# Two chained blocks on one core: 80 units of the modulation taken from the matrix engine and computed beside the feed-forwards

## The chip, the core and the metric

The kernel runs on one core of a Trainium2 chip. Five things work side by side in it: TensorE (PE, with its weight loads as PEld), VectorE (DVE), ScalarE (ACT), GpSimd (POOL, unused here), and the DMA queues, of which SyncE's (SP) brings nearly all weights. The metric is the device time of one execution in microseconds (us); lower is better.

## What is computed

256 tokens of width 1024 pass through two blocks, one after the other, in fp32.

```python
def first_block(x, ...):                 # two layers
    for layer in range(2):
        p = rms_norm(h, g1) @ w_in       # split into branch A, B, C and gates
        y_a = rwkv7_branch(p_a, ...)     # a recurrence, computed in chunks
        y_b = hgrn2_branch(p_b, ...)
        y_c = dsa_branch(p_c, ...)
        branch = einsum('bsnc,ncd->bsnd', [y_a, y_b, y_c], w_branch)
        h = h + (sum over n of sigmoid(p_gate) * branch) @ w_o
        u = rms_norm(h, g2)
        h = h + conv_glu(u, w_up, conv_w, conv_b, w_down)    # width 2816

def second_block(x, c, ...):             # two layers
    cond = silu(c)                       # one vector of 1024
    for layer in range(2):
        mod = cond @ ada_w[layer] + ada_b[layer]             # 1024 x 6144
        sh1, sc1, g1, sh2, sc2, g2 = split(mod, 6)
        h = rms_norm(x, ...) * (1 + sc1) + sh1
        x = x + g1 * hybrid_mixer(h, ...)  # GLA (log_a = f(ga @ w_alpha)) and retention
        h = rms_norm(x, ...) * (1 + sc2) + sh2
        x = x + g2 * (swiglu(h) if layer == 0 else moe_swiglu(h))  # 8 experts, top 2
    return rms_norm(x, final_g)
```

The product `cond @ ada_w` needs nothing of the first block: it can be made anywhere before the second block starts.

## The kernel before

**Products.** An fp32 product is made of three matmuls on rounded halves: w_high × u_high, w_high × u_low and w_low × u_high. The weights come in units of 128 x 1024 (512 KB). A unit of 8 K-tiles and 128 outputs takes 24 matmuls of 128x256. SyncE brings each unit into one of `RING` = 6 slots; ScalarE rounds it to `w_high` (`high_to`, L1744), VectorE subtracts (`low_to`, L2275, `w_low`), and TensorE multiplies (`project`, `mm3`, all recorded at L801). The halves live in 6 slots of their own (`SPLIT`), so a unit can be cut up to 6 ahead of its product. SyncE issues the loads in the order of the list `ORDER.loads`, and waits before each until the slot's former unit has been read: for a split unit by VectorE's cut, for a raw one ("r") by TensorE's product. Every engine runs its own program in the order in which it is written, and the waits are on semaphores that the others count up.

**The modulation.** `ada_w` of both layers is 96 units. TensorE multiplies them raw, in plain fp32, 48 in branch A of each layer of the first block (`mod_point`, L897). There A runs through some fifty short products of 64x64 tiles, each of which depends on the copies of the one before; at each `point()` four units stand between, with two matmuls of 512 columns for each (rows "bank<-ring,cond"). The results stand in PSUM bank 7. After 16 units (a round of `Rounds`) ScalarE copies the bank, TensorE transposes it at the next point ("const,rope"), and ScalarE takes 16 columns of `mod` out of it. At the end of branch B VectorE copies `mod` to `raw_mod`.

**Merge.** `branch(n, ...)` multiplies the outputs of A, B and C with 4 units each, 0 in banks 0 to 3, 1 and 2 both in banks 4 to 7; branch n's results are multiplied with gate n by VectorE ("taken", "merged") before their bank is free. Branch 2 waits for `gated` (VectorE), its high half (ScalarE, `high_y2`) and its low half (`cut2`). The units of w_o follow, in banks 0 to 7 in order, four of them interleaved by `begin`, and the sums of squares for the next norm.

**Feed-forward.** There are 22 groups of two up units (gate, value) and one down unit. Units are numbered in TensorE's order: `feed(j, n, groups)`; TensorE runs up of group j and then down of group j − 2. ScalarE and VectorE start group j with cutting up to `fed_ahead(j)` = 3j + 4 (5 for j = 0). In a conv group ScalarE then takes gate and value with the first tap (L2065, L2066), VectorE adds the two other taps (4 instructions, L2316), ScalarE makes the sigmoid (L2068), VectorE the two products (L2307), ScalarE `hid_high` (L2074) and VectorE `hid_low`. The third dense feed-forward (second block, layer 0) has no taps. At the end ScalarE cuts three units of the next stage (`ahead`), loads an activation table (L1777) and squares the new residual (L1780) for the norm, which TensorE sums.

**GLA.** `ga`, 16 columns of the projection, is made of 16 thin fp32 matmuls from constant weights ("const 128*16"). VectorE copies it, and TensorE makes `alpha` of it.

## Time and profile before

| | |
|---|---|
| median of 3 runs | 2419.52 us (2409.2 to 2420.85) |
| the profiled execution, its own time | 2427.1 us |
| its span in the profile | 2425.6 us |
| mean granted TensorE clock | 0.962 of full speed |
| busy: TensorE / VectorE / ScalarE | 2269.0 / 1601.5 / 1174.7 us |
| instructions: PE matmul / DVE / ACT | 19011 / 2442 / 1703 |

The profile comes from one execution, so its times are compared with each other and with its own total. A row of the timeline gives start, duration, engine, line and operation, and in brackets how long the engine had been idle before and what released it. "issue" is idle time for which nothing that the profile shows was waited for.

### The profile page before, as it was taken

How to read it: one execution, taken by the hardware profiler on the slowest of the kernel's cores; microseconds unless marked ns; L12 is line 12 of the kernel's file. 1: busy time of each engine (PE TensorE's matmuls, PEld its weight loads, DVE VectorE, ACT ScalarE, POOL GpSimd, SP SyncE). 2: the span in 40 equal slices, each digit the busy share in tenths (PEclk: the TensorE clock that was granted, in tenths of full speed). 3: DMA queues.
4: the chain of work that ended last, by engine and by line, in shares of the span. 5: the costliest groups of instructions: out<-in, count | busy, mean ns of one | idle time of the engine just before them, and what ended most of it. 6: DMA issues, size and time to landing. Idle time of an engine off the chain costs nothing.

```text
span 2425.6 us, 44884 instructions
## 1 busy us (share of the span) xinstructions
PE 2269.0 (94%) x19011; PEld 2047.3 (84%) x19011; DVE 1601.5 (66%) x2442; ACT 1174.7 (48%) x1703; POOL 0.2 (0%) x4
## 2 busy tenths in 40 slices
PE   7889998999998898989999989999989999999998
PEld 7569888999976798988998989998987888877776
DVE  6537976677673589576876666555666454577886
ACT  5234644555452455355554445444345344456665
POOL 0000000000000000000000000000000000000000
PEclk9999998999899999899998989999998999999999
DMA  5664433365447543253653325553313555579885
GB/s 209 229 252 165 139 122 121 114 200 198 137 163 256 206 138 123 88 172 123 205 188 130 131 82 179 184 187 130 126 36 133 180 200 176 175 278 321 328 319 198
DMA packets 118635, 427.06 MB, mean 176 GB/s; under 512 B 13345, under 2 KB 16161, under 8 KB 118305
## 3 DMA queue, kind: packets, MB, share of 16 engines
q1 hardware_dynamic: 116016, 421.81, 50.3%
q8 instruction: 150, 2.46, 0.4%
q10 hardware_dynamic: 2416, 2.37, 0.3%
q14 instruction: 53, 0.43, 0.1%
HBM read 423.08 MB, written 1.05 MB: 175 GB/s over the span
## 4 chain that ended last, share of the span: by engine, by line
PE 80%; DVE 11%; ACT 4%; issue 2%; DMA 2%; SPq 0%; ACTq 0%; DVEq 0%
PE bank L801 79%; DVE arena L2307 3%; DVE w_low L2275 3%; DMA ring<-in_weights 2%; DVE arena L2316 1%; ACT w_high L1744 1%; DVE y_mix L2307 1%; ACT arena L2024 1%; PE bank L1629 1%; DVE arena L2326 0%; DVE arena L2311 0%; PE bank L949 0%; DVE x_res L2316 0%; ACT arena L1750 0%; DVE u_low L2307 0%
## 5 line engine op out<-in xcount | busy, mean ns | idle before, releaser
L2275 DVE TENSOR_TENSOR w_low<-ring,w_high 128x1024 fp32r<-128x1024 f32 x700 | 822.9, 1219 | 144.9 <-ACT w_high L1744 143.9
L801 PE MATMUL bank<-u_high,w_high 128*128 128x256 f32 x2576 | 742.4, 288 | 36.8 <-DVE u_low L2307 19.7
L1744 ACT ACTIVATE w_high<-ring 128x1024 fp32r<-128x1024 f32 x700 | 700.9, 1051 | 134.4 <-PE bank L801 124.3
L801 PE MATMUL bank<-u_low,w_high 128*128 128x256 f32 x2576 | 734.1, 285 | 0.0
L801 PE MATMUL bank<-u_high,w_low 128*128 128x256 f32 x2576 | 733.5, 285 | 0.0
L801 PEld LDWEIGHTS bank<-u_high,w_high 128*128 128x128 f32 x2576 | 498.8, 194 | 50.8 <-issue 35.0
L801 PEld LDWEIGHTS bank<-u_low,w_high 128*128 128x128 f32 x2576 | 498.6, 194 | 0.1
L801 PEld LDWEIGHTS bank<-u_high,w_low 128*128 128x128 f32 x2576 | 497.8, 193 | 0.0
L801 PE MATMUL bank<-arena 64*64 64x64 f32 (+5 forms) x4456 | 232.8, 248 | 43.2 <-issue 21.5
L801 PEld LDWEIGHTS bank<-arena 64*64 64x64 f32 (+2 forms) x4456 | 204.0, 152 | 79.7 <-issue 57.1
L801 PE MATMUL bank<-w_high,u_high 128*128 128x256 f32 (+1 forms) x480 | 165.2, 344 | 0.0
L801 PE MATMUL bank<-w_low,u_high 128*128 128x256 f32 (+1 forms) x480 | 162.3, 338 | 0.0
L2307 DVE TENSOR_TENSOR arena<-arena 128x256 f32<-128x256 f32 (+3 forms) x218 | 141.8, 666 | 31.0 <-ACT arena L2068 21.3
L801 PE MATMUL bank<-w_high,u_low 128*128 128x256 f32 (+1 forms) x480 | 162.2, 338 | 0.0
L801 PE MATMUL bank<-hid_high,w_high 128*128 128x256 f32 x528 | 148.1, 280 | 1.0 <-DVE w_low L2275 1.0
L801 PE MATMUL bank<-hid_low,w_high 128*128 128x256 f32 x528 | 147.9, 280 | 0.0
L801 PE MATMUL bank<-hid_high,w_low 128*128 128x256 f32 x528 | 147.9, 280 | 0.0
L2307 DVE TENSOR_TENSOR turned_low<-bank,turned_high 128x256 fp32r<-128x256 f32 (+1 forms) x66 | 24.8, 399 | 158.3 <-ACT turned_high L2180 158.3
L2180 ACT ACTIVATE turned_high<-bank 128x256 fp32r<-128x256 f32 (+1 forms) x66 | 22.2, 365 | 218.3 <-PE bank L1629 218.3
L2316 DVE SCALAR_TENSOR_TENSOR arena<-bank,params,arena 128x255 f32<-128x255 f32 (+1 forms) x204 | 85.4, 475 | 39.7 <-ACT arena L2066 23.3
L1750 ACT ACTIVATE arena<-bank 128x512 f32<-128x512 f32 (+1 forms) x72 | 42.0, 583 | 138.2 <-PE bank L801 138.1
L801 PE MATMUL bank<-w_high,turned_high 128*128 128x512 f32 x242 | 99.7, 412 | 8.3 <-DVE w_low L2275 7.0
(307 smaller groups left out, 3062.7 us busy)
## 6 DMA issues: line engine op xcount, KB each, us to landing
ring<-in_weights SPq DMA_DIRECT2D x534, 512.0 KB, 4.5
ring<-in_moe SPq DMA_DIRECT2D x264, 512.0 KB, 5.2
const<-in_const SPq DMA_DIRECT2D x1, 2619.0 KB, 16.7
out<-x_res ACTq DMA_DIRECT2D x2, 512.0 KB, 3.0
x_res<-in_x SPq DMA_DIRECT2D x1, 512.0 KB, 5.1
x_res<-in_x ACTq DMA_DIRECT2D x1, 512.0 KB, 5.6
const<-in_par ACTq DMA_DIRECT2D x1, 462.0 KB, 3.4
params<-in_par ACTq DMA_DIRECT2D x1, 247.0 KB, 10.3
```

What stands on the lines that cost most here:

```text
L801: return pe.matmul(out, lhsT, rhs, start=start, stop=stop, skip_group_check=loose)
L1629: ins = pe.transpose(bank(q, tile)[:, f * P:(f + 1) * P], hid_e[q % 2][tile][:, f * P:(f + 1) * P], c_("ident"))
L1744: act.activation(WH[:, ORDER.slot[cut], :], weights("s", cut), Copy).then_inc(s_hi, 1)
L1750: act.activation(job.dst, held(job), Copy).then_inc(s_out["act"], 1)
L2024: act.activation(L_c[a][:, h, :], L_c[a][:, h, :], Exp, bias=neg_max[a][:, h:h + 1], accum_out=exp_sum[a][:, h:h + 1]).then_inc(*c.mark(f" ...
L2180: act.activation(HTH[q % 2][tile][:, 0:n], psum[4 + 2 * (q % 2) + tile][:, 0:n], Copy)\
L2275: dve.tensor_tensor(WL[:, b, :], weights("s", cut), WH[:, b, :].bitcast(f32), SUB).then_inc(s_lo, 1)
L2307: dve.tensor_tensor(out, a, b, op).then_inc(*t.mark(name))
L2316: dve.scalar_tensor_tensor(out, a, s, b, op0, op1).then_inc(*t.mark(name))
```

## The change

1. Of the 96 units of the modulation only round 0 of layer 0 (16 units) stays on TensorE in branch A; layer 1's A has none. The other 80 are laid out by result: a row of 128 x 1024 holds 128 columns' weights, one column to a partition. `ROWS` gives 20, 20 and 40 of them to the three dense feed-forwards. From group 3 on VectorE multiplies such a row with `cond_row` (the vector cond in all partitions) and ScalarE sums it up with a copy and `accum_out` into a column of `raw_mod`. Each of the three loads c, broadcast, as one unit more (kind "m"), and makes `cond_row` of it in groups 1 and 2. The slot of a row is free when VectorE's product is made.
2. In a conv group both engines have a new order. ScalarE: gate and value with taps, two highs, sigmoid, one high, `hid_high`, the sum of the group before. VectorE: taps, one low, the two products, one low, `hid_low`, one low, the modulation's product. In the third feed-forward the old order stays, and the rows' products stand ahead of `hid_low`.
3. Merge: branch 2 goes to banks 0 to 3, the units of branch 2 are cut further before its input is ready, gate 2 stands ahead of `high_y2`, and w_o goes to the banks `MIXED_BANK` = (7, 4, 5, 6, 0, 1, 2, 3), after `taken13`.
4. GLA: `ga` becomes a unit like the others (24 matmuls, a load and both cuts), the first in the mixer; `alpha` follows directly on VectorE's copy, and the other projection jobs come after it.

```diff
+    ROUNDS1 = range(0, 1), range(1, 1)
+    ROWS = range(16, 36), range(36, 56), range(56, 2 * MOD_UNITS)
+    GA2, QK2, RQK2, RV2, GV2, GR2, RG2, OUT2, FEED2 = 0, 1, 5, 13, 17, 21, 25, 29, 37
...
+    def _feed(self, g, first):
+        for j in range(FF_GROUPS):
+            before, last = self.fed_ahead(j - 1, FF_GROUPS) if j else -1, self.fed_ahead(j, FF_GROUPS)
+            self._load("s", first + before + 1, last - before)
+            of = self.modulated(g, j)
+            self._load("m", self.row1(g) + of[0] if len(of) else 0, len(of))
+
+    def modulated(self, g, j):
+        n = len(self.ROWS[g])
+        if j < 3:
+            return range(j == 1)
+        return range(1 + n * (j - 3) // (FF_GROUPS - 3), 1 + n * (j - 2) // (FF_GROUPS - 3))
...
                     if m == 0:
                         pe.wait_ge(*G.dve(f"cut{n}"))
+                        if n == 2:
+                            pe.wait_ge(*B.dve("gated"))
                     pe.wait_ge(s_lo, s + 1)
                     for dt in range(KT):
-                        if m == 0 and n == 2 and dt % 2 == 0:
-                            pe.wait_ge(*G.dve(f"taken1{dt // 2}"))
-                        ins = mm3(half((0, 4, 4)[n] + dt // 2, dt), halves(s, slice(dt * P, (dt + 1) * P)),
+                        ins = mm3(half((0, 4, 0)[n] + dt // 2, dt), halves(s, slice(dt * P, (dt + 1) * P)),
...
+            pe.wait_ge(*G.dve("taken13"))
+            begin(G.dve, [(s + dt, psum[MIXED_BANK[dt]][:, 0:T], True) for dt in range(4)])
+            projected_out(s, R, MIXED_BANK)
...
             high_to(s0 + ORDER.BRANCH + 7)
+            gate(2)
+            high_to(s0 + ORDER.BRANCH + 9)
             act.wait_ge(*B.dve("gated"))
             act.activation(YH[2], OUTS[2], Copy).then_inc(*g.mark("high_y2"))
-            gate(2)
...
+            def row(j):
+                K, at = of_rows[g], ORDER.row1(g)
+                if j == 1:
+                    act.wait_ge(*arrived("m", at))
+                    act.activation(cond_row, weights("m", at), Sigmoid).then_inc(*K.act.mark("cond"))
+                for i in ORDER.modulated(g, j) if j > 2 else ():
+                    act.wait_ge(*K.dve(f"product{i}"))
+                    col = ORDER.ROWS[g][i - 1]
+                    act.activation(products[i % 3], products[i % 3], Copy, accum_out=raw_mod[:, col:col + 1])\
+                        .then_inc(*K.act.mark(f"sum{i}"))
...
-                high_to(s0 + ORDER.fed_ahead(j, groups))
+                if conv is None or j == 0:
+                    high_to(s0 + ORDER.fed_ahead(j, groups))
...
+                    high_to(s0 + ORDER.fed_ahead(j, groups) - 1)
                     act.wait_ge(*F[j].dve("read"))
                     act.activation(SG[n], CG[n], Sigmoid).then_inc(*f.mark("sig"))
+                    high_to(s0 + ORDER.fed_ahead(j, groups))
...
                 act.activation(HH[:, ts_], HD[n], Copy).then_inc(*f.mark("high"))
+                row(1 if j == 1 else j - 1 if j > 3 else 0)
...
+            row(groups - 1)
             if ahead:
                 high_to(s0 + 3 * groups + 2)
...
+                for i in ORDER.modulated(g, j) if j > 2 else ():
+                    dve.wait_ge(*arrived("m", at + i))
+                    if i > 3:
+                        dve.wait_ge(*K.act(f"sum{i - 3}"))
+                    tt(K.dve, products[i % 3], weights("m", at + i), cond_row, MUL, f"product{i}")
...
+                    low_to(s0 + ORDER.fed_ahead(j, groups) - 2)
                     dve.wait_ge(*F[j].act("sig"))
                     tt(f, SG[n], SG[n], CG[n], MUL)
...
+                if conv is None:
+                    row(j)
+                else:
+                    low_to(s0 + ORDER.fed_ahead(j, groups) - 1)
                 dve.wait_ge(*F[j].act("high"))
                 tt(f, HL[:, ts_], HD[n], HH[:, ts_].bitcast(f32), SUB, "hidden")
+                if conv is not None:
+                    low_to(s0 + ORDER.fed_ahead(j, groups))
+                    row(j)
...
-            for k in range(KT):
-                for part in (UH, UL):
-                    ins = mm(psum[0][0:16, 0:T], wga[:, k, :], part[:, k, :].bitcast(f32),
-                             k == 0 and part is UH, k == KT - 1 and part is UL)
-            ins.then_inc(*L.pe.mark("ga"))
-            fill(side, 1)
             pe.wait_ge(*L.dve("ga"))
...
+                if old == "m":
+                    g = sum(was >= ORDER.row1(n) for n in (1, 2))
+                    was -= ORDER.row1(g)
+                    sp.wait_ge(*of_rows[g].dve(f"product{was}" if was else "cond"))
```

The order on three engines, before and after. TensorE, branch A of layer 1, just behind the products with the low-rank weights: `arena,const` are products with constants, `arena 64x64` the chain of small products, and `ring,cond` is a unit of the modulation. Before:

```order
L801 MATMUL bank<-arena,const 128x256 [waits s_a_act,s_a_dve]
L801 MATMUL bank<-arena,const 128x256 x3
L801 MATMUL bank<-ring,cond 32x512 [waits s_slot3,s_a_dve]
L801 MATMUL bank<-ring,cond 32x512
L801 MATMUL bank<-ring,cond 32x512 [waits s_slot4]
L801 MATMUL bank<-ring,cond 32x512
L801 MATMUL bank<-ring,cond 32x512 [waits s_slot5]
L801 MATMUL bank<-ring,cond 32x512
L801 MATMUL bank<-ring,cond 32x512 [waits s_slot0]
L801 MATMUL bank<-ring,cond 32x512
L801 MATMUL bank<-arena,const 128x256 [waits s_a_dve]
```

and of the change:

```order
L847 MATMUL bank<-arena,const 128x256 [waits s_a_act,s_a_dve]
L847 MATMUL bank<-arena,const 128x256 x3
L847 MATMUL bank<-arena,const 128x256 [waits s_a_dve]
L847 MATMUL bank<-arena,const 128x256 x3
L847 MATMUL bank<-arena 64x64 [waits s_a_dve]
L847 MATMUL bank<-arena 64x64 x63
L995 MATMUL bank<-const,arena 128x128 x4
L847 MATMUL bank<-arena 64x64 [waits s_a_act,s_a_dve]
L847 MATMUL bank<-arena 64x64 x31
```

The `arena,const` products are followed by the chain of 64x64 products, and no row of layer 1 has `ring,cond` any more.

VectorE, start of the first feed-forward, from group 0's two products on; `w_low` are the cuts. Before:

```order
L2307 TENSOR_TENSOR arena<-arena 128x256 [waits s_conv_act]
L2307 TENSOR_TENSOR arena<-arena 128x256 [waits s_conv_dve]
L2307 TENSOR_TENSOR hid_low<-arena,hid_high 128x256 [waits s_conv_act]
L2275 TENSOR_TENSOR w_low<-ring,w_high 128x1024 [waits s_high_halves] x2
L2316 SCALAR_TENSOR_TENSOR arena<-bank,params,arena 128x255 [waits s_conv_act]
L2316 SCALAR_TENSOR_TENSOR arena<-bank,params,arena 128x255
L2316 SCALAR_TENSOR_TENSOR arena<-bank,params,arena 128x254 [waits s_conv_dve] x2
L2307 TENSOR_TENSOR arena<-arena 128x256 [waits s_conv_act]
L2307 TENSOR_TENSOR arena<-arena 128x256 [waits s_conv_dve]
L2307 TENSOR_TENSOR hid_low<-arena,hid_high 128x256 [waits s_conv_act]
```

and of the change:

```order
L2368 TENSOR_TENSOR arena<-arena 128x256 [waits s_conv_act]
L2368 TENSOR_TENSOR arena<-arena 128x256 [waits s_conv_dve]
L2368 TENSOR_TENSOR hid_low<-arena,hid_high 128x256 [waits s_conv_act]
L2377 SCALAR_TENSOR_TENSOR arena<-bank,params,arena 128x255 [waits s_conv_act]
L2377 SCALAR_TENSOR_TENSOR arena<-bank,params,arena 128x255
L2377 SCALAR_TENSOR_TENSOR arena<-bank,params,arena 128x254 [waits s_conv_dve] x2
L2368 TENSOR_TENSOR arena<-arena 128x256 [waits s_conv_act]
L2368 TENSOR_TENSOR arena<-arena 128x256 [waits s_conv_dve]
L2336 TENSOR_TENSOR w_low<-ring,w_high 128x1024 [waits s_high_halves]
L2368 TENSOR_TENSOR hid_low<-arena,hid_high 128x256 [waits s_conv_act]
L2336 TENSOR_TENSOR w_low<-ring,w_high 128x1024 [waits s_high_halves]
```

The two cuts that stood behind group 0's `hid_low` (units 6 and 7) stand behind group 1's taps and products now.

ScalarE, end of the first feed-forward, from `hid_high` of the last group but one or the taps of the last on, to the squares of the next norm. Before:

```order
L2068 ACTIVATE arena<-arena 128x256 [waits s_conv_dve]
L2074 ACTIVATE hid_high<-arena 128x256 [waits s_units_multiplied,s_conv_dve]
L1744 ACTIVATE w_high<-ring 128x1024 [waits s_units_multiplied,s_slot0]
L1744 ACTIVATE w_high<-ring 128x1024 [waits s_units_multiplied,s_slot1]
L1744 ACTIVATE w_high<-ring 128x1024 [waits s_units_multiplied,s_slot2]
L1777 ACT_TABLE_LOAD
L1777 ACTIVATE steady<-steady 128x1
L1780 ACTIVATE arena<-x_res 128x256 [waits s_add_dve] x8
```

and of the change:

```order
L2125 ACTIVATE arena<-arena 128x256 [waits s_conv_dve]
L1786 ACTIVATE w_high<-ring 128x1024 [waits s_units_multiplied,s_slot4]
L2132 ACTIVATE hid_high<-arena 128x256 [waits s_units_multiplied,s_conv_dve]
L2107 ACTIVATE arena,raw_mod<-arena 128x1024 [waits s_rows_dve] x3
L1786 ACTIVATE w_high<-ring 128x1024 [waits s_units_multiplied,s_slot1]
L1786 ACTIVATE w_high<-ring 128x1024 [waits s_units_multiplied,s_slot2]
L1786 ACTIVATE w_high<-ring 128x1024 [waits s_units_multiplied,s_slot3]
L1819 ACT_TABLE_LOAD
L1819 ACTIVATE steady<-steady 128x1
L1822 ACTIVATE arena<-x_res 128x256 [waits s_add_dve] x8
```

Three sums of the modulation (`arena,raw_mod`) stand between the last `hid_high` and the three early cuts.

## Rows read from the trace of the kernel before

**Rows 1.** The page: span, busy time by engine, chain that ended last, instruction queue.

```profile
span 2425.6 us, 44884 instructions
PE 2269.0 (94%) x19011; PEld 2047.3 (84%) x19011; DVE 1601.5 (66%) x2442; ACT 1174.7 (48%) x1703; POOL 0.2 (0%) x4
...
q8 instruction: 150, 2.46, 0.4%
...
PE 80%; DVE 11%; ACT 4%; issue 2%; DMA 2%; SPq 0%; ACTq 0%; DVEq 0%
```

**Rows 2.** Windows: stretch, length, busy of PE PEld DVE ACT POOL, clock, DMA share, GB/s.

```profile
64.90:175.20 110.30, 93.11 (x2132) 63.97 (x2133) 40.88 (x77) 25.79 (x47) 0.00 (x0) 0.94 0.67 247
170.00:175.00 5.00, 4.09 (x117) 3.79 (x111) 1.09 (x5) 1.01 (x4) 0.00 (x0) 0.66 0.02 3
706.10:815.30 109.20, 91.35 (x2132) 61.02 (x2133) 40.87 (x77) 25.77 (x47) 0.00 (x0) 0.95 0.68 251
555.00:640.00 85.00, 85.00 (x727) 85.00 (x726) 63.49 (x103) 45.08 (x68) 0.00 (x0) 1.00 0.56 190
1500.00:1550.00 50.00, 50.00 (x424) 50.00 (x423) 29.32 (x37) 23.25 (x30) 0.00 (x0) 1.00 0.60 193
2200.00:2250.00 50.00, 48.52 (x216) 37.17 (x214) 39.40 (x43) 33.12 (x43) 0.00 (x0) 1.00 0.88 318
```

**Rows 3.** Lines on PE, branch A, layer 1 (705.5:815.5): busy, mean | idle before, releasers.

```profile
L801 PE MATMUL bank<-arena 64*64 64x64 f32 (+1 forms) x1760 | 48.7, 224 | 11.6 <-issue 10.8 <-DVE arena L2307 0.5 <-PE bank L801 0.2
L801 PE MATMUL bank<-ring,cond 128*32 128x512 f32 x192 | 32.7, 663 | 6.8 <-DMA ring<-in_weights 3.4 <-DVE arena L2307 2.6 <-ACT mod L1824 0.8
...
L902 PE MATMUL bank<-const,rope 128*128 128x128 f32 x12 | 2.0, 286 | 1.2 <-ACT rope L1819 1.2
```

**Rows 4.** Timeline on PE, both branches A: start, duration, operation, [idle before <-releaser].

```profile
94.12 1.72 PE L801 MATMUL bank<-arena 64*64 64x64 f32 x38 [2.34 <-issue]
...
106.92 2.08 PE L801 MATMUL bank<-arena 64*64 64x64 f32 x62 [1.56 <-issue]
...
723.63 1.67 PE L801 MATMUL bank<-arena 64*64 64x64 f32 x49 [1.23 <-issue]
...
734.27 0.39 PE L801 MATMUL bank<-arena 64*64 64x64 f32 x6 [1.84 <-issue]
```

**Rows 5.** Lines on PE, branch A, layer 0, 104:165.

```profile
L801 PE MATMUL bank<-ring,cond 128*32 128x512 f32 x128 | 19.4, 600 | 2.7 <-DMA ring<-in_weights 1.9 <-ACT mod L1824 0.8
```

**Rows 6.** Timeline on PE: merge of layer 0, and GLA's gate of layer 0.

```profile
410.45 0.55 PE L801 MATMUL bank<-y_high,w_high 128*128 128x256 f32 x1 [4.92 <-DVE y_mix L2307]
...
426.14 0.36 PE L801 MATMUL bank<-u_high,w_high 128*128 128x256 f32 x1 [1.41 <-DVE u_low L2307]
...
1315.34 0.60 PE L801 MATMUL bank<-u_high,const 128*16 128x256 f32 x2
...
1322.35 0.39 PE L801 MATMUL bank<-u_high,w_high 128*128 128x256 f32 x1
```

**Rows 7.** Timeline on PE: start of the first feed-forward.

```profile
475.54 0.38 PE L801 MATMUL bank<-hid_high,w_high 128*128 128x256 f32 x1 [0.49 <-DVE w_low L2275]
```

**Rows 8.** Lines on DVE, inside the first feed-forward, 555:640.

```profile
L2275 DVE TENSOR_TENSOR w_low<-ring,w_high 128x1024 fp32r<-128x1024 f32 x29 | 33.9, 1220 | 5.2 <-ACT w_high L1744 5.2
L2316 DVE SCALAR_TENSOR_TENSOR arena<-bank,params,arena 128x255 f32<-128x255 f32 (+1 forms) x44 | 18.2, 475 | 6.2 <-ACT arena L2066 6.2
L2307 DVE TENSOR_TENSOR arena<-arena 128x256 f32<-128x256 f32 x20 | 8.5, 425 | 5.2 <-ACT arena L2068 4.8
L2307 DVE TENSOR_TENSOR hid_low<-arena,hid_high 128x256 fp32r<-128x256 f32 x10 | 4.3, 426 | 4.8 <-ACT hid_high L2074 4.8
```

**Rows 9.** Timeline on ACT and PE: end of the first feed-forward.

```profile
641.88 2.94 ACT L1744 ACTIVATE w_high<-ring 128x1024 fp32r<-128x1024 f32 x3
...
646.70 5.91 PE L801 MATMUL bank<-steady,arena 128*128 128x1 f32 x32 [0.84 <-ACT arena L1780]
```

**Rows 10.** Lines on ACT, whole span: reading an accumulated sum.

```profile
L2024 ACT ACTIVATION_READ_ACCUMULATOR arena<-arena,small 128x1 f32 x32 | 6.0, 187 | 0.0
```

More of the change, by code:

```diff
@@ L111, in constants, with __init__, more, out @@
     return c
+class Rounds:
+    ROUND = 2 * KT
+    def __init__(self, rounds):
+        self.first, self.last = rounds.start, rounds.stop
+        self.taken, self.stage = self.ROUND * self.first, 3 * self.first
+    def more(self, n):
+        r, at = self.stage // 3, self.stage % 3
+        if at == 1:
+            self.stage += 1
+            return r, True, range(0)
+        if at:
+            return r, False, range(0)
+        first, self.taken = self.taken, min(self.taken + n, (r + 1) * self.ROUND, self.last * self.ROUND)
+        return r, False, range(first, self.taken)
+    def out(self):
+        r, at = self.stage // 3, self.stage % 3
+        if (at == 0 and self.taken == (r + 1) * self.ROUND) or at == 2:
+            self.stage += 1
+            return r, at
+        return r, None
+    def open(self):
+        return self.stage < 3 * self.last
 class Order:
@@ L677, in build @@
     CG, CV, SG, HD = ([new(T) for _ in TWO] for _ in range(4))
+    cond_row, products = at(32 * T, 4 * T), [at((36 + 4 * n) * T, 4 * T) for n in range(3)]
     space(0)
@@ L3180, in modulation @@
             d = S.dve
+            for n in (0, 1) if layer == 0 else (2,):
+                dve.wait_ge(*of_rows[n].act.end())
+            if layer == 0:
+                dve.wait_ge(*of_mod.act("out"))
             tt(d, mod, raw_mod[:, layer * MOD_UNITS:(layer + 1) * MOD_UNITS], par2(layer, "ada_b"), ADD)
```

160 lines of the change are left out of this document (81 added, 79 removed), and 13 rows, old and new, of the table STEPS.

## The prediction

> **What bounds the kernel now.** I read the page first, then windows by stage, then the groups of TensorE inside the windows that the change touches, then single instructions at the joints between stages. TensorE is busy for 94% of the span, and the chain that ended last runs through it for 80% [rows 1]. VectorE is busy 66% and ScalarE 48%, but that is an average. In the feed-forwards TensorE has no idle time at all (85.00 of 85 us, 50.00 of 50), while VectorE rests for a quarter or more of the time and the DMA share is 0.56 to 0.60 [rows 2]. In the two stages of branch A TensorE still issues over 2,100 instructions, and is busy 93.11 of 110.30 and 91.35 of 109.20 us [rows 2]. So a multiplication taken out of A comes off the path, and the same work put on VectorE and ScalarE beside a feed-forward should cost nothing as long as a group stays below TensorE's own 8.42 us: 727 matmuls in 85 us are 0.117 us each, 72 to a group, 10.1 groups [rows 2].
>
> **Modulation out of A of layer 1.** All 192 matmuls from ring and cond go: 32.7 us, with 3.4 of waits for their loads and 0.8 for ScalarE [rows 3]. So do the three turns, 2.0 and 1.2 of waiting [rows 3]. Together 40.1 us. These points stood where the dependent chain of A (one 64x64 product, a copy, the next) would otherwise have shown its waits for VectorE and ScalarE. They hid them: the group of 64x64 products waits only 0.5 us for VectorE [rows 3]. I place the exposed waits at about 9 us in all (3.3 before the first products, 0.3 to 0.9 at some seven further steps and tails), an estimate from the lengths of the copies between products. That leaves −31 us.
>
> There is a second limit. 10.8 us of A's idle time is put down to issue, with no wait behind it [rows 3]. These gaps return every 10.64 us (723.63 to 734.27) [rows 4], and between two of them lie 256 matmuls and their 256 weight loads. The page's instruction queue fits that: 150 packets of 2.46 MB, one for 127 of the 19,011 pairs [rows 1], so two packets to a period. If TensorE can't go through A faster than one period for each 256 matmuls, the 2132 − 192 − 12 = 1928 that stay need 7.5 × 10.64 = 80.1 us instead of 109.2: −29. Both accounts agree nearly; I take −29, with −40 (nothing exposed) and −16 (the slower period, below) as ends.
>
> The Trainium skill, "Runtime: NRT & Kernel Launch", section "Instruction fetch mechanics", says that crossing an instruction block is mostly hidden by the issue of instructions. Here the trace disagrees in A: 10.8 us stand there as idle with no releaser [rows 3]. By the page alone no floor would exist, and the gaps would have another cause.
>
> **The same in layer 0.** Only round 0 stays (16 units at the first four points, and one turn). 128 records go, 19.4 us with 2.7 of waits [rows 5], and two of the three turns, about 2: 24 us. Exposed waits are some 4, since the first points keep their cover: −20. The gaps are worse in this layer: 12.80 us from 94.12 to 106.92 [rows 4]. I take −19, ends −12 and −24.
>
> Denser products were also what held the clock up: both windows were granted 0.94 and 0.95 [rows 2]. From 170 to 175 us, where A has no such products left, it is 0.66 [rows 2]: TensorE is then for a part of the time at 1.2 instead of 2.4 GHz. With the 512-column products gone such stretches can come more often. I allow +4 for both layers (0 to +10).
>
> **Merge.** Branch 2 starts after 4.92 us of waiting for VectorE's gated output, and w_o after 1.41 more [rows 6]. Between the two 14.28 us (410.45 to 426.14 less 1.41) go for 96 matmuls, 11.2 at 0.117. The change lets VectorE and ScalarE cut units of branch 2 ahead of that output, and puts branch 2 into banks that are free. By my sum w_o starts at about 421 instead of 426, but what bounds it then is VectorE's chain of taken and merged products, so that TensorE's wait moves to w_o's head and is not gone. −5.2 a layer if the clock holds, −2.2 if the 3 us of low clock stay: −3.5 each, −7.
>
> **GLA's gate unit.** The 16 thin fp32 matmuls take 1315.34 to 1322.35, 7.0 us [rows 6]; as a split unit they are 24 × 0.117 = 2.8. The alpha product now waits for VectorE's copies with nothing between, about 1.2. −3 a layer, −6 (−4 to −8). The extra load and cuts (1.0 on ScalarE, 1.2 on VectorE) fall where both have slack.
>
> **Feed-forwards, the start.** The first down unit (its wait for w_low was 0.49) [rows 7] is now cut after the taps and both products of group 1. I place its cut 3.5 us after TensorE is ready; later waits of 0.8 and some 3.4 (layer 1) mostly go. +2.5 in all.
>
> **Feed-forwards, inside.** VectorE's work of a conv group is (33.9 + 18.2 + 8.5 + 4.3) / 10.1 = 6.43 us, and it waits (5.2 + 6.2 + 5.2 + 4.8) / 10.1 = 2.1 [rows 8]. A product costs as much as a cut of the same shape, 1.22: 7.65 of 8.42. It fits only because the new order puts a cut into each of the waits for the sigmoid and for hid_high, so that they overlap with work. ScalarE goes from 45.08 / 10.1 = 4.5 to 5.7. The third feed-forward has 29.32 / 50 × 8.42 = 4.9 [rows 2] plus 2.1 products = 7.5. The loads rise from three units a group to four (five in the third, 5.1 × 0.524 MB / 8.42 us = 318 GB/s). The experts show just that rate, 318 GB/s with TensorE 48.52 of 50 busy [rows 2], so the rings should stand it. Cost 0, up to +8.
>
> **Feed-forwards, the end.** This cost isn't covered. On ScalarE the last three sums now stand ahead of the three early highs (641.88, 2.94 us), the table load and the squares for the next norm [rows 9]. Two of them wait for products that VectorE makes after hid_low: 0.5 + 2 × 1.22 + 1.2 (1.0 as for a high, and 0.19 to read the accumulator [rows 10]) = 4.1, with semaphores and the third sum about 5.5. TensorE's 32 thin sums of squares at 646.70 wait for ScalarE already, 0.84 [rows 9], and nothing else is queued behind the last down product. So all 5.5 is on the path, for each conv feed-forward. The third has five sums, three behind late products: +5. Total +16 (+6 if the products run ahead, +20).
>
> **Sum.** −29 −19 +4 −7 −6 +2.5 +0 +16 = −38.5. Against the profiled run of 2427.1 us (span 2425.6 [rows 1]) that is 2388.6. The median of the runs is 7.6 lower, so 2419.5 − 38.5 = **2381 us**.
>
> **Rivals.**
> *Instruction supply is slower than I take it.* The period was 12.80 us in layer 0 [rows 4]. If it is 12.5 where nothing pads it, A of layer 1 takes 7.5 × 12.5 = 94 (−15) and A of layer 0 saves 12: 18 + 3 worse in the two, and with the clock term doubled 2381 + 25 = 2406. For it: it is the same kind of code, and nothing in the profile says why it is slower there. Against it: the 10.64 us of layer 1 [rows 4], beside the same DMA traffic (0.68 and 0.67) [rows 2]. Chance 0.14.
> *The ends cost less or A gains more.* If VectorE is ahead by a group at the ends, or the gaps shrink with the ring's traffic gone from A, −16 to −20 more: 2363. For the second: A's ring traffic of 250 GB/s [rows 2] goes with the modulation. Against it: a gap has no releaser among the DMAs [rows 3]. Chance 0.2.
> *The feed-forwards become VectorE's.* The one that ends slower. If the waits of 2.1 us stay beside 7.65 of work, a conv group takes 9.75, 1.3 more, × 38 groups = +50; the third, with some 1.9 of waits on 7.5, +1 × 19 = +19. A late load of a product's row also holds up SP's queue, in which every load stands in order, and the slot comes free only with VectorE's product. 2381 + 69 = 2450. It decides from 38.5 / 57 = 0.68 us a group (no gain), and is slower by 0.5% from 50.6 / 57 = 0.9. Against it: of the three waits two now have a cut of 1.2 in front of them, longer than the waits were. Chance 0.04.
> *The same, by half* (0.3 to 0.6 a group), or the clock falls through both A: about 2412. Chance 0.07.
> *Forecast*: 0.55.
>
> **Numbers.** The range takes in the ends of the likeliest case and the two neighbours: 2360 to 2407; what is left out is about 0.13 above and 0.07 below. 0.5% is 12 us, about what a measurement of this kernel tells from no change: faster means below 2407.4, slower above 2431.6. Faster 0.87, same 0.09, slower 0.04.
>
> **What would show it.** A of layer 1 at 78 to 84 us with issue gaps every 10.6 us and no ring and cond matmuls; 94 if the supply is slower. A of layer 0 near 91. Windows inside the feed-forwards still at 50.00 of 50 on TensorE with VectorE about 0.9 busy; any idle there released by w_low or hid_low speaks for the third rival, by a ring slot for its second half. At the end of each feed-forward a TensorE wait of 5 to 6 us for squares, where 0.84 stood. w_o's first matmul waiting 3 to 5 us for u_low. GLA's gate at 4 us up to alpha. The prediction is wrong at its base if TensorE's matmuls of a feed-forward take more than 0.117 us each beside the denser traffic.

## The result, and the profile after

The changed kernel takes 2363.99 us (median of 4 runs, 2360.04 to 2367.22), the kernel before 2420.18 (4 runs): 0.9769, 95% interval 0.9747 to 0.9791. That is 56 us, where 38.5 were forecast (2381 us, with a range from 2360 to 2407). The profiled execution took 2361.86 us, its span is 65.2 us shorter than that of before.

The page of the changed kernel: span, busy time, chain that ended last.

```profile
span 2360.4 us, 44488 instructions
PE 2206.9 (93%) x18655; PEld 2036.3 (86%) x18655; DVE 1683.8 (71%) x2525; ACT 1253.7 (53%) x1858; POOL 0.2 (0%) x4
...
PE 82%; DVE 12%; ACT 4%; issue 2%; DMA 1%; ACTq 0%; DVEq 0%; SPq 0%
```

TensorE's busy time falls by 62.1 us, VectorE's rises by 82.3 and ScalarE's by 79.0, and the chain still runs through TensorE. Windows of the changed kernel (columns as in [rows 2]): A of layer 0, A of layer 1, inside the first and inside the third feed-forward, and the sums of squares behind the first.

```profile
64.36:149.70 85.34, 71.12 (x1996) 57.29 (x1996) 40.70 (x77) 24.50 (x43) 0.00 (x0) 0.96 0.33 123
679.40:751.50 72.10, 61.53 (x1946) 56.06 (x1945) 45.52 (x90) 27.78 (x46) 0.00 (x0) 0.95 0.11 40
500.00:600.00 100.00, 100.00 (x845) 100.00 (x844) 86.04 (x131) 66.59 (x107) 0.00 (x0) 1.00 0.75 247
1450.00:1580.00 130.00, 130.00 (x1110) 130.00 (x1109) 108.74 (x125) 89.55 (x141) 0.00 (x0) 1.00 0.92 324
624.00:632.00 8.00, 7.03 (x33) 6.94 (x33) 0.74 (x2) 2.77 (x10) 0.00 (x0) 0.50 0.54 183
```

The first two answer to the first and third of [rows 2]. In A of layer 1 the DMA share went from 0.68 to 0.11, and the matmuls that are left take 72.1 us. Inside the feed-forwards TensorE is as busy as it was, with VectorE at 86% (75% before, 63.49 of 85), and in the third the loads run at 324 GB/s.

The stages, each from the same landmark to the same landmark on TensorE's timeline in both traces:

| stage | before | after | difference | forecast |
|---|---|---|---|---|
| A of layer 0 (from the low-rank products to those of y_mix) | 115.4 | 90.5 | −24.9 | −17 with the clock's share |
| A of layer 1 | 114.4 | 72.1 | −42.3 | −27 with the clock's share |
| B, C and merge, two layers | 532.5 | 522.6 | −9.8 | −7 |
| conv feed-forwards with their norms, two layers | 428.6 | 444.8 | +16.2 | +13.5 |
| third feed-forward | 197.3 | 200.6 | +3.3 | +5 |
| both GLA mixers | 330.8 | 323.7 | −7.1 | −6 |
| all else | 706.6 | 706.1 | −0.5 | 0 |
| span | 2425.6 | 2360.4 | −65.2 | −38.5 |

The table compares one trace with one trace. The changed kernel was traced once more (the last of the experiments); there the six stages took 91.9, 72.2, 523.6, 448.2, 200.8 and 319.7 us. So both A repeat within 1.4 us, while the conv feed-forwards differ by 3.4 and the GLA mixers by 4.0 between executions of the same code.

Nearly all of what was missed stands in branch A. Its groups on TensorE, first layer 1 and then layer 0 (busy, mean ns | idle before, releasers), answering to [rows 3] and [rows 5]:

```profile
L847 PE MATMUL bank<-arena 64*64 64x64 f32 (+1 forms) x1760 | 47.6, 225 | 4.4 <-DVE arena L2368 1.8 <-issue 1.3 <-DVE arena L2380 0.8
```

```profile
L847 PE MATMUL bank<-arena 64*64 64x64 f32 (+1 forms) x1760 | 50.0, 225 | 10.3 <-issue 7.5 <-DVE arena L2368 1.6 <-DVE arena L2380 0.8
L847 PE MATMUL bank<-ring,cond 128*32 128x512 f32 x64 | 11.4, 692 | 4.7 <-DVE arena L2368 2.6 <-DMA ring<-in_weights 2.1
```

In layer 1 the idle time of issue fell from 10.8 to 1.3 us; in layer 0, where round 0 still streams through the ring, it is 7.5 (10.7 before). What the chain of small products waits for now, in layer 1, is 1.8 + 0.8 us of VectorE where it was 0.5.

The joints between stages on TensorE: w_o of the first merge, the first down unit, the squares behind the three feed-forwards, the products behind GLA's gate.

```profile
394.99 0.55 PE L847 MATMUL bank<-u_high,w_high 128*128 128x256 f32 x1 [3.72 <-DVE u_low L2368]
...
447.48 0.39 PE L847 MATMUL bank<-hid_high,w_high 128*128 128x256 f32 x1 [3.39 <-DVE w_low L2336]
...
624.42 6.99 PE L847 MATMUL bank<-steady,arena 128*128 128x1 f32 x32 [5.04 <-ACT arena L1822]
...
1228.78 6.96 PE L847 MATMUL bank<-both,arena 128*128 128x2 f32 x32 [5.12 <-ACT arena L1822]
...
1257.22 1.13 PE L847 MATMUL bank<-arena,const 16*128 16x256 f32 x4 [1.10 <-DVE arena L2380]
...
1591.19 5.77 PE L847 MATMUL bank<-steady,arena 128*128 128x1 f32 x32 [2.59 <-ACT arena L1822]
```

### The profile page after: what moved, and what is told of

It is laid out like the page before. It is cut to its first block, busy times and chain, and to the rows that moved or that the text cites. A ratio compares the mean times of both kernels' runs of the same rounds, so it can differ in the third digit from the quotient of the medians.

```text
span 2360.4 us, 44488 instructions
## 1 busy us (share of the span) xinstructions
PE 2206.9 (93%) x18655; PEld 2036.3 (86%) x18655; DVE 1683.8 (71%) x2525; ACT 1253.7 (53%) x1858; POOL 0.2 (0%) x4
## 4 chain that ended last, share of the span: by engine, by line
PE 82%; DVE 12%; ACT 4%; issue 2%; DMA 1%; ACTq 0%; DVEq 0%; SPq 0%
PE bank L847 80%; DVE arena L2368 4%; DVE w_low L2336 3%; ACT w_high L1786 1%; DVE arena L2377 1%; DVE y_mix L2368 1%; ACT arena L2066 1%; PE bank L1669 1%; DVE arena L2387 0%; PE bank L995 0%; DVE arena L2380 0%; DMA ring<-in_weights 0%; DVE arena L2372 0%; ACT arena L1792 0%; DVE u_low L2368 0%
## 5 line engine op out<-in xcount | busy, mean ns | idle before, releaser
L847 PE MATMUL bank<-u_high,w_high 128*128 128x256 f32 x2592 | 749.0, 289 | 36.1 <-DVE u_low L2368 24.9
L1786 ACT ACTIVATE w_high<-ring 128x1024 fp32r<-128x1024 f32 x702 | 705.5, 1052 | 104.1 <-PE bank L847 92.8
L847 PEld LDWEIGHTS bank<-u_high,w_high 128*128 128x128 f32 x2592 | 504.1, 194 | 48.2 <-issue 31.3
L847 PEld LDWEIGHTS bank<-u_low,w_high 128*128 128x128 f32 x2592 | 504.4, 195 | 0.1
L847 PEld LDWEIGHTS bank<-u_high,w_low 128*128 128x128 f32 x2592 | 502.9, 194 | 0.0
L2368 DVE TENSOR_TENSOR arena<-arena 128x256 f32<-128x256 f32 (+3 forms) x218 | 141.6, 665 | 13.5 <-ACT arena L2081 4.7
L2368 DVE TENSOR_TENSOR turned_low<-bank,turned_high 128x256 fp32r<-128x256 f32 (+1 forms) x66 | 24.9, 400 | 159.6 <-ACT turned_high L2240 159.6
L847 PEld LDWEIGHTS bank<-hid_high,w_high 128*128 128x128 f32 x528 | 100.4, 190 | 9.3 <-DVE w_low L2336 8.7
```

Of the source, the lines that this page charges most:

```text
L847: return pe.matmul(out, lhsT, rhs, start=start, stop=stop, skip_group_check=loose)
L1786: act.activation(WH[:, ORDER.slot[cut], :], weights("s", cut), Copy).then_inc(s_hi, 1)
L2368: dve.tensor_tensor(out, a, b, op).then_inc(*t.mark(name))
```

## The experiments

**Traffic without modulation.** The changed kernel with loads in A of layer 1 that nobody reads:

```diff
             self._load("r", self.raw1(layer) + 1, Rounds.ROUND * len(self.ROUNDS1[layer]))
+            if layer == 1:
+                self._load("x", 0, 40)
...
-                if old == "m":
+                if old == "x":
+                    sp.wait_ge(s_slot[n % RING], 16 * (n // RING))
+                elif old == "m":
```

> The changed kernel, with 40 loads of 512 KB put into the ring in branch A of layer 1, where nothing is left of the modulation's traffic. No engine reads them: each slot is loaded again as soon as its own load has landed. Theory 1 (the gaps of issue come from the ring's traffic, which holds up TensorE's instructions): issue idle in A of layer 1 rises from 1.3 us back to 9 to 13, and A goes from 72.1 us to 80 to 85. Theory 2 (the gaps hang on the modulation's matmuls or on something else of the kernel before): issue stays under 3 us, A at 72 to 74. Outside A of layer 1 both expect what the changed kernel has.

The run took 2380.1 us, and its span is 18.2 us above the changed kernel's, all of it in A of layer 1, which took 90.3 us (679.27 to 769.54) instead of 72.1. Its main group on TensorE:

```profile
L849 PE MATMUL bank<-arena 64*64 64x64 f32 (+1 forms) x1760 | 53.5, 234 | 16.4 <-issue 13.3 <-DVE arena L2370 1.8 <-DVE arena L2382 0.8
```

13.3 us of issue, with not one matmul more. Most of the rest is in the same matmuls (53.5 us busy instead of 47.6), beside a lower granted clock: 0.88 and 0.86 from 700 to 740, where the changed kernel has 1.00. Windows of this run across A of layer 1; the loads end at about 740:

```profile
680.00:700.00 20.00, 12.56 (x275) 10.15 (x275) 17.93 (x29) 9.22 (x13) 0.00 (x0) 0.83 0.91 354
700.00:720.00 20.00, 14.31 (x416) 13.43 (x417) 5.02 (x7) 4.76 (x8) 0.00 (x0) 0.88 1.03 407
720.00:740.00 20.00, 15.95 (x422) 14.93 (x420) 8.93 (x13) 2.97 (x5) 0.00 (x0) 0.86 1.03 408
740.00:770.00 30.00, 24.88 (x846) 22.67 (x842) 13.08 (x39) 10.68 (x19) 0.00 (x0) 1.00 0.04 15
```

and of the changed kernel:

```profile
680.00:700.00 20.00, 14.89 (x367) 12.31 (x367) 18.97 (x32) 9.97 (x15) 0.00 (x0) 0.83 0.36 133
700.00:720.00 20.00, 19.22 (x680) 18.61 (x677) 12.92 (x18) 5.36 (x9) 0.00 (x0) 1.00 0.02 4
720.00:751.00 31.00, 26.82 (x912) 24.57 (x907) 12.66 (x39) 11.58 (x22) 0.00 (x0) 1.00 0.02 4
```

From 700 to 720 us this run goes through 416 matmuls beside 407 GB/s, the changed kernel through 680 beside 4 GB/s. The two windows don't hold the same matmuls, but counted on the same ones it is no different: the 831 that this run needed 40 us for (700 to 740) took the changed kernel 25.0 (697.7 to 722.6); as soon as the loads end, 846 follow in 30 us, close to the changed kernel's 912 in 31. The queues in that stretch of the run with loads (packets, MB, share of 16 engines):

```profile
q1 hardware_dynamic: 2223, 8.09, 101.7%
q8 instruction: 3, 0.05, 1.0%
```

Three instruction packets in 20 us, one for 6.2 to 6.7, and the gaps of issue come back every 6.2 us (706.29, 712.48, 718.70, 724.90, 731.17). The start and duration of each packet in the trace tie the two together. In this stretch the packets start at 703.74, 709.97, 716.20, 722.46 and 728.70 and last 1.1 us each, and every gap ends 1.3 to 1.5 us after one has landed. The same holds for all 32 gaps of issue above 0.3 us in eight stretches of branch A: both of the kernel before and of the changed kernel, layer 1 of this run, of the next one and of the changed kernel's second trace, and layer 0 of the run with all units as rows. Each gap ends 1.2 to 1.6 us after the landing of an instruction packet, and from one gap to the next lie 127 or 128 matmuls or a multiple of that. So the gaps are waits for instructions. Beside the loads the packets come 6.2 us apart; without them they come 3.5 apart (changed kernel, 698.53, 702.27, 705.75, 709.22, 712.72) and, from 700 to 720, no gap shows. A packet itself lasts 1.1 us there and 0.9 to 1.1 here, so what the loads lengthen is the time from one packet to the next.

Theory 1 holds. The size was more than it asked for (90.3 us, where 80 to 85 were expected), under a traffic that was heavier than the modulation's mean of 251 GB/s.

**Modulation without traffic**, the reverse, in the kernel before:

```diff
-            self._load("r", layer * self.RAW1 + 1, MOD_UNITS)
+            if layer == 0:
+                self._load("r", layer * self.RAW1 + 1, MOD_UNITS)
...
-                pe.wait_ge(*arrived("r", raw))
+                if layer == 0:
+                    pe.wait_ge(*arrived("r", raw))
+                    unit = weights("r", raw)
+                else:
+                    unit = const[:, P:P + 1024]
```

> The kernel before, with the 48 units of the modulation of layer 1 multiplied as before (192 matmuls of 512 columns at the same points), but from a constant region and with no loads; layer 1's modulation is set to its bias alone, so that part of the result is left out. Theory 1 (traffic makes the gaps): of the 109.2 us from 706.1 to 815.3, the 3.4 us of waits for loads go and issue falls from 10.8 to under 3: 96 to 98 us. Theory 2 (the matmuls of the modulation make the gaps): only the 3.4 go, 105 to 106 us, issue 9 to 12. The floor of my prediction (256 matmuls in 10.64 us whatever else runs) expects the same as theory 2.

This run leaves layer 1's modulation out of the result. It took 2395.1 us. A took 91.8 us from the low-rank products on (699.99 to 791.74), where the kernel before took 114.4; over the stretch of the expectation (109.2 us before) it is 86.6, where theory 1 expected 96 to 98. Its groups on TensorE:

```profile
L802 PE MATMUL bank<-arena 64*64 64x64 f32 (+1 forms) x1760 | 47.0, 222 | 1.7 <-issue 0.9 <-DVE arena L2312 0.5 <-PE bank L802 0.2
L802 PE MATMUL bank<-const,cond 128*32 128x512 f32 x192 | 24.6, 634 | 3.4 <-DVE arena L2312 2.6 <-ACT mod L1829 0.8
```

All 192 wide matmuls are there and issue is 0.9 us. −22.6 is more than theory 1's 11 to 13: beside the 9.9 us of issue and 3.4 of waits for loads, the wide matmuls themselves take 24.6 us busy instead of 32.7 [rows 3]. The timelines show where these 8.1 us were. Four units in a row in the kernel before, and four in this run:

```profile
757.46 1.49 PE L801 MATMUL bank<-ring,cond 128*32 128x512 f32 x8
759.15 1.05 PE L801 MATMUL bank<-ring,cond 128*32 128x512 f32 x4 [0.20 <-DMA ring<-in_weights]
760.41 1.05 PE L801 MATMUL bank<-ring,cond 128*32 128x512 f32 x4 [0.21 <-DMA ring<-in_weights]
...
746.11 1.92 PE L802 MATMUL bank<-const,cond 128*32 128x512 f32 x16
```

Without loads the four matmuls of a unit always start within 0.02 us of each other. In the kernel before, 14 of the 48 units start the second two 0.18 to 0.85 us after the first two, and 12 of these 14 begin within 0.06 us of the landing of a load (9 of the other 34 do). Over all units the time from the first of the four starts to the last is 8.3 us before and 1.0 here. So most of the 8.1 us stands in units whose matmuls ran one pair after the other, mostly units whose load had only just landed: a cost of late loads that the idle time doesn't show. Why the pairs don't start together then, no run here separates.

**The order inside a conv group.**

```diff
-                if conv is None or j == 0:
-                    high_to(s0 + ORDER.fed_ahead(j, groups))
+                high_to(s0 + ORDER.fed_ahead(j, groups))
...
-                if conv is None or j == 0:
-                    low_to(s0 + ORDER.fed_ahead(j, groups))
+                low_to(s0 + ORDER.fed_ahead(j, groups))
```

> The changed kernel with the order of before in the conv groups: every group first cuts up to its last unit on both engines and then takes taps, sigmoid, products and halves; the rows' product and sum stand where they are. By my account VectorE's cycle of a group with a product is 7.65 of work and 2.1 of waits, 9.75 instead of 8.42 of TensorE: 38 groups x 1.3 = +50 us (2410 to 2415). If the waits shrink when VectorE is late (its partners are then done), the cycle is 8.4 to 8.8: 0 to +15 us. The wait of 3.4 us at the first down unit goes in either case, twice.

2381.0 us in one run, where 2410 to 2415 or up to 15 above the changed kernel were expected. From the first sums of squares behind w_o to the squares behind the feed-forward it took 225.0 and 227.7 us, the changed kernel 213.8 and 215.6. TensorE's timeline inside the first:

```profile
513.41 0.38 PE L847 MATMUL bank<-u_high,w_high 128*128 128x256 f32 x1 [0.18 <-DVE w_low L2335]
...
522.31 0.38 PE L847 MATMUL bank<-u_high,w_high 128*128 128x256 f32 x1 [0.18 <-DVE w_low L2335]
```

The groups are 8.90 us apart, 0.48 more than TensorE's own 8.42, and each waits for w_low. VectorE's groups in the same feed-forward (500:610):

```profile
L2335 DVE TENSOR_TENSOR w_low<-ring,w_high 128x1024 fp32r<-128x1024 f32 x36 | 42.0, 1221 | 5.2 <-ACT w_high L1786 5.2
L2376 DVE SCALAR_TENSOR_TENSOR arena<-bank,params,arena 128x255 f32<-128x255 f32 (+1 forms) x48 | 19.7, 474 | 0.0
L2367 DVE TENSOR_TENSOR arena<-arena 128x256 f32<-128x256 f32 x26 | 11.0, 425 | 6.7 <-ACT arena L2124 6.3
L2367 DVE TENSOR_TENSOR hid_low<-arena,hid_high 128x256 fp32r<-128x256 f32 x13 | 5.5, 425 | 6.3 <-ACT hid_high L2131 6.3
```

Its waits shrank, from 2.1 us to (5.2 + 6.7 + 6.3) / 12.4 = 1.5 a group (893 matmuls, 72 to a group), and the wait for the taps is gone. So the order is needed, but what it saves is 11 to 12 us a feed-forward with the joints, not 25: the waits shrink when VectorE is late, as the second half of the expectation says.

**Merge as before**: banks, `taken` waits, gate 2 and the cuts of branch 2 put back.

```diff
-                        if n == 2:
-                            pe.wait_ge(*B.dve("gated"))
...
+                        if m == 0 and n == 2 and dt % 2 == 0:
+                            pe.wait_ge(*G.dve(f"taken1{dt // 2}"))
-                        ins = mm3(half((0, 4, 0)[n] + dt // 2, dt),
+                        ins = mm3(half((0, 4, 4)[n] + dt // 2, dt),
...
-    MIXED_BANK = (7, 4, 5, 6, 0, 1, 2, 3)
+    MIXED_BANK = (0, 1, 2, 3, 4, 5, 6, 7)
```

> The changed kernel with merge's banks and its order of before, all else as changed. From the y_mix products behind A to the first sum of squares behind w_o the changed kernel took 260.9 and 261.7 us, that of before 265.4 and 267.1. If merge alone makes the difference: 265 to 266 and 266 to 267, some 10 us more in all (2371 to 2376). If a part came from clock or from branches B and C: under +3 each.

2372.7 us in one run; the stage took 265.9 and 263.8 us, 5.0 and 2.1 above the changed kernel's. The first is as expected, the second less than half: 7 us in all, and the stage varies by 2 us between executions of the same code (262.3 and 260.6 in layer 1 of the runs with the old order and with traffic). The run without loads has merge as before, and there the stage took 264.1 and 262.7. So merge is worth some 7 us, as forecast, and 4 with that run in place of the kernel before; that it is 10 isn't shown.

**The rows end at group 19.**

```diff
-        return range(1 + n * (j - 3) // (FF_GROUPS - 3), 1 + n * (j - 2) // (FF_GROUPS - 3))
+        first, last = (1 + n * (min(i, FF_GROUPS - 2) - 3) // (FF_GROUPS - 5) for i in (j, j + 1))
+        return range(first, last)
```

> The changed kernel with the rows of each feed-forward spread over groups 3 to 19 instead of 3 to 21, so that ScalarE has no sum behind the last hid_high. If the sums at the end are what TensorE's wait for squares is made of: 5.04, 5.12 and 2.59 us go back to 0.8 to 0.9 (third: 0), and the sums of squares behind them run at the pace of before; -5 per conv feed-forward and -3 to -5 for the third, -13 in all. Rival: 40 rows over 17 groups are 5.35 loads for 8.42 us of TensorE, 333 GB/s, where the changed kernel has 324 at a DMA share of 0.92: the third is then bound by its loads and gets 2 to 6 us longer inside, which takes its gain back: -8.

2341.8 us (2335.6 to 2349.6), ratio 0.9687 (0.9653 to 0.9721): 22 us below the changed kernel's 2364.0, where 13 were expected. To see what went away, first ScalarE in the changed kernel behind the first feed-forward's last hid_high:

```profile
617.42 1.06 ACT L2107 ACTIVATE arena<-arena 128x1024 f32<-128x1024 f32 x1 [1.72 <-DVE arena L2368]
618.39 0.18 ACT L2107 ACTIVATION_READ_ACCUMULATOR arena<-arena 128x1 f32 x1
618.55 1.06 ACT L2107 ACTIVATE arena<-arena 128x1024 f32<-128x1024 f32 x1
619.52 0.18 ACT L2107 ACTIVATION_READ_ACCUMULATOR arena<-arena 128x1 f32 x1
619.61 2.94 ACT L1786 ACTIVATE w_high<-ring 128x1024 fp32r<-128x1024 f32 x3
622.57 1.28 ACT L1819 ACT_TABLE_LOAD   x1
```

Three sums stand there. The first, at 614.56, isn't shown; the second comes after 1.72 us of waiting for VectorE's product. They all stand before the three highs, the table load and the squares. With the rows ended at group 19 TensorE's end of the same stage reads:

```profile
612.39 0.39 PE L848 MATMUL bank<-hid_high,w_high 128*128 128x256 f32 x1 [0.59 <-DVE w_low L2337]
...
615.46 4.81 PE L848 MATMUL bank<-steady,arena 128*128 128x1 f32 x31
```

There is no wait in front of the sums of squares, and all 32 take 5.0 us instead of 7.0 (the row has 31 of them), behind the second feed-forward 3.7. In the changed kernel, behind the 5 us of idle time, TensorE was granted 0.50 (1.2 GHz) for all of them, as the window 624:632 above shows. From the norm before it to the norm behind it, the first feed-forward lasted 200.0 us (208.7 in the changed kernel), the second 205.1 (210.7), the third 196.3 (200.6): −18.7. My expectation had named the pace of the squares and counted too little for it. The span of this trace is 26.3 us shorter; the rest stands mainly in B, C and merge (−4.3) and in GLA (−6.1), which the edit doesn't touch, and the four executions of this kernel range over 14 us. So the edit is shown to be worth 19 and not all of the 22. The rival is refuted: from 1430 to 1560 the third ran at 334 GB/s with TensorE busy for all 130 us.

**The start.** The old order in group 1 of the conv feed-forwards.

```diff
-                if conv is None or j == 0:
+                if conv is None or j < 2:
```

> The changed kernel with the old order in group 1 of the conv feed-forwards too (both engines cut up to unit 7 before the taps of group 1). The wait of 3.39 us before the first down unit goes back to 0.4 to 0.5 in both; stalls of 0.8 to 1.8 a little later may come back, as the kernel before and the old order had them. -6 if none comes back, -2 if they do.

2365.1 us, ratio 0.9778 (0.9753 to 0.9803): nothing gained, where 2 to 6 us were expected. TensorE in the first feed-forward:

```profile
441.96 0.38 PE L847 MATMUL bank<-hid_high,w_high 128*128 128x256 f32 x1 [0.43 <-DVE w_low L2336]
...
451.15 0.58 PE L847 MATMUL bank<-u_high,w_high 128*128 128x256 f32 x1 [3.23 <-DVE w_low L2336]
```

The first down unit no longer waits, and an up unit of group 3 does, for the same time. VectorE is some 3 us behind once at the start, and the order only chooses who waits.

**All 96 units as rows** (28, 28 and 40).

```diff
-    ROUNDS1 = range(0, 1), range(1, 1)
-    ROWS = range(16, 36), range(36, 56), range(56, 2 * MOD_UNITS)
+    ROUNDS1 = range(0, 0), range(0, 0)
+    ROWS = range(0, 28), range(28, 56), range(56, 2 * MOD_UNITS)
```

> The changed kernel with all 96 units of the modulation as rows: 28, 28 and 40, none left on TensorE in A of layer 0 and no ring traffic for it. Theory 1 (traffic makes the gaps): A of layer 0 goes from 85.4 to about 72 us, as layer 1 has it, issue from 7.5 to 1 to 2. By matmuls alone, without the gaps, 85.4 - 11.4 - 0.7 - 2.1 + 4 = 75 to 76. VectorE has 6.43 + 28/19 x 1.22 = 8.2 us of work for a conv group of 8.42, and one more sum at the end of some: 0 to +3 for each conv feed-forward if it still fits, +10 if it does not. In all -13 to -7, or +5 if it does not fit.

2341.7 us (2337.1 to 2349.0), ratio 0.9669 (0.9644 to 0.9694). It is 22 us below the changed kernel, where 7 to 13 were expected. A of layer 0 took 71.9 us (60.29 to 132.19), 18.6 less than in the changed kernel; the expectation had counted 13, because it took 85.4 us for A of layer 0, a stretch that starts 5 us later than the 72 us of layer 1:

```profile
L845 PE MATMUL bank<-arena 64*64 64x64 f32 (+1 forms) x1760 | 46.9, 223 | 5.0 <-DVE arena L2366 2.9 <-issue 1.0 <-DVE arena L2378 0.8
```

1.0 us of issue, as theory 1 says. The conv feed-forwards cost 3.2 and 1.7 us more, about what was expected for a VectorE that still fits (0 to 3).

**Start and end together**, the third feed-forward left as changed.

```diff
+        last = FF_GROUPS if g == 2 else FF_GROUPS - 2
+        of = [1 + n * (min(i, last) - 3) // (last - 3) for i in (j, j + 1)]
+        return range(*of)
...
-                if conv is None or j == 0:
+                if conv is None or j < 2:
```

> The changed kernel with the conv feed-forwards' rows over groups 3 to 19 and the old order in their group 1; the third feed-forward as changed. If both effects add and stay apart: 2 x (5 + 1 + 2 to 3) = -15 to -18, 2346 to 2350 where the changed kernel has 2364. If stalls come back at the start: -12.

2346.6 us (2345.7 to 2350.2), ratio 0.970 (0.9676 to 0.9725): −17, as expected. The conv ends gain and the start adds nothing: the first feed-forward took 203.5 us, and 200.0 with the ends alone.

**The best version**: all 96 units as rows, and the rows in groups 3 to 19, beside the changed kernel on the same chip.

> All 96 units as rows (28, 28, 40) and the rows over groups 3 to 19: the two edits that gained alone. If they add: A of layer 0 at 72 us (-18 against the changed kernel) and the ends without a wait for squares (-13 to -19): 2364 - 33 = 2325 to 2333. Against: VectorE has 6.43 + 28/17 x 1.22 = 8.44 us of work for a conv group, as much as TensorE takes (8.35 to 8.44), so that it can fall behind: +0 to +4 in all.

> The changed kernel once more, unchanged, on the same chip as the combined version, so that the two stand side by side: 2360 to 2369 us, 0.975 to 0.979 of the kernel before. Also for the pace of TensorE inside the feed-forwards, which was 845 matmuls in 100 us in this kernel's trace and 854 in that with the rows over groups 3 to 19: if the pace belongs to the kernel, 845 again; if it varies between executions, anything from 842 to 856.

2325.7 us (2314.5 to 2328.0), ratio 0.9595 (0.9559 to 0.9631), and the changed kernel beside it 2366.2 us, 0.977 (0.974 to 0.980). The two edits nearly add up: −40.5, where the two alone gave −22 each and 33 were expected in all. A of layer 0 and the inside of the first feed-forward in the combined version:

```profile
59.50:131.00 71.50, 59.97 (x1947) 54.81 (x1945) 45.32 (x89) 27.80 (x46) 0.00 (x0) 0.98 0.11 40
500.00:600.00 100.00, 100.00 (x845) 100.00 (x844) 91.91 (x137) 73.47 (x121) 0.00 (x0) 1.00 0.84 283
```

VectorE is at 92% there and TensorE has no idle time. The changed kernel's own pace in its second trace was 854 matmuls in 100 us where the first had 845, so this 1% belongs to the execution and not to the kernel. Nor is it the chip: of the traces taken on one chip, that of all rows has 845 and that of the rows ended at group 19 has 854.

## Why the prediction was right, and where it was wrong

**The sign and the bound** were right: work taken from TensorE's path and given to engines with slack in a stage where TensorE is the bound. **The size** was 17.5 us short (56 for 38.5). The measured 2364 is the value of the second rival (2363), which had a chance of 0.2, and the range holds it by 4 us, only because it reached down to that rival. The likeliest account, with A at its floor, didn't come true.

**Modulation out of A: mis-sized, and for a wrong reason.** The step that failed is the "second limit", a floor of 10.64 us for 256 matmuls, from which −29 was taken. With −29, A of layer 1 would have taken 85.4 of the table's 114.4 us; it took 72.1. A of layer 0 was to stand near 91 for the 110.3 of [rows 2]; it took 85.3. The gross sum of 40.1 us was right, and my 9 us of exposed waits were too many: 1.3 + 0.8 us more of VectorE, 0.7 of ScalarE, 1.7 more of waiting and some 1.8 of low clock at the first products are between 6 and 7.
The Trainium skill, "Runtime: NRT & Kernel Launch", section "Instruction fetch mechanics", says that the sequencer fetches its next page through a DMA queue of its own. The trace agrees that there is such a queue: q8 stands beside the weights' q1, and under the loads its packets came 6.2 us apart instead of 3.5. Its "mostly hidden" holds at 40 GB/s of other traffic in A (1.3 us of issue) and not at 251 GB/s (10.8) or more (13.3).

**The same in layer 0**: −24.9 against −19. 128 matmuls and two turns were costed right; the gaps fell by 3.2 us, only in part, since round 0 kept its traffic, and the exposed waits were under 3 us instead of 4.

**The clock**: +4 was allowed, and over the whole of A nothing shows: 0.96 and 0.95 after, 0.94 and 0.95 before. What came is the 1.8 us at the first products, counted above. So the wide products were not what held the clock up in A as a whole, as the prediction had it: layer 1 has none left and was granted 0.95. What idle time came with the exposed waits is less than what went with the gaps; that this is why the clock held is argued and not shown.

**Merge**: −9.8 in the traces, 7 by the run that puts it back, −7 forecast, where executions differ by some 2 us a layer. w_o's first matmul waits 3.72 us for u_low, as predicted (3 to 5), and branch 2 no longer waits.

**GLA's gate**: −7.1 against −6, the wait for VectorE's copy 1.10 us as against 1.2. The second mixer gave only 1.1 of it (163.4 us for 164.5), but in the changed kernel's second trace it took 158.9, so this belongs to the one execution: from its norm to the products behind the gate TensorE was granted 0.79 there, 0.85 in the second trace and 0.89 before. By the second trace GLA is worth 11.

**Feed-forward, start**: 3.39 us against 3.5 forecast, in both. **Inside**: cost 0, as forecast; the third rival, a feed-forward bound by VectorE, would have come with the old order, at 0.48 us a group instead of my 1.3. **End**: the waits for squares are 5.04 and 5.12 us, 4.2 more than before, and the sums behind them take 1.1 us more at the lower clock level (6.99 for 5.91), which I hadn't thought of: 5.3 each, for 5.5 forecast: near in number, but with less waiting than forecast and a clock term that the forecast didn't have. In the third the wait is 2.59 and the stage 3.3 longer, for 5 forecast.

So A, with its allowance for the clock, was 23 us off, and every other term within 3 us; merge and GLA make the rest of the 26.7 us between the traces' 65.2 and the forecast. The medians differ by 56 only, because the profiled execution of before was 7 us above its median and that of after 2 below.

## What to carry to other kernels

Before moving work off a dense stage, look at what its loads do to the others in that stage, and at the fetching of instructions first: in a stage of many short instructions, DMA traffic is a cost of its own, and idle time under "issue" beside a high DMA share is its sign. Put streaming work beside long matmuls, which need few instructions for each microsecond. Work that is fitted into an engine's slack should end some groups before the stage does, since what follows its last piece on that engine is on the path, and the stage behind it starts at the lower clock.

## What the runs showed of the hardware

- Under 407 GB/s of loads TensorE got one instruction packet in 6.2 us, without them one in 3.5; its chain of short products then took 40 us for what it does in 25. At 251 GB/s the gaps were 10.8 us in 109.
- All 32 gaps of issue above 0.3 us in eight stretches of branch A end 1.2 to 1.6 us after the landing of an instruction packet of 16 KB.
- 192 matmuls of 512 columns from a constant region were 24.6 us busy with no loads beside them, 32.7 from the ring; most of the difference stands in 14 units of 48 whose four matmuls didn't start together.
- In the feed-forwards, loads at up to 334 GB/s (DMA share 0.94) cost TensorE nothing that shows. There a packet lasts for 127 pairs of 0.117 us.
- An idle time of 5 us in front of 32 thin matmuls was followed by a granted clock of 0.50 through all of them (6.99 us). Behind 0.84 us of idle time they took 5.91 us at 0.60, behind 2.6 us 5.8 in one trace of the changed kernel and 6.9 in the other.
- The pace inside a feed-forward differs by 1% (845 or 854 matmuls in 100 us) between layers and executions of one kernel, at a granted clock of 1.00. Its cause stays open.
